# Low parts of the gate weights in the RWKV phase: subtraction moved from POOL to DVE

## The reference

```python
a_q, a_k, a_v, a_f, b_q, b_k, b_v, c_in, gate_in = _split_cols(h @ w_in, IN_SPLITS)
...
y_c, s_new = _rwkv7_scan(heads(cr), heads(decay), heads(kmod), heads(cv), kk, heads(a), rwkv_s0)
...
branches = jnp.stack([out_a, out_b, out_c], axis=2)
proj = jnp.einsum('btiw,iwd->btid', branches, w_branch)
gates = jax.nn.sigmoid(gate_in.reshape(b, t, N_BRANCH, D_MODEL))
y = jnp.sum(gates * proj, axis=2) @ w_out
```

## Time and profile before

| what | value |
|---|---|
| median of 3 runs | 3753.3 us (3747.02 to 3755.54) |
| the profiled execution | 3756.2 us, its span 3754.6 us |
| busy share of the span | PE 83%, PEld 75%, DVE 43%, ACT 18%, POOL 9% |
| mean granted PE clock | 0.866 of full speed |
| RWKV phase, first layer | from about 727 to 1093 us of the span |
| RWKV phase, second layer | from about 2574 to 2939 us |

### The profile page before, as it was taken

The page is one execution under the profiler, slowest core; times in us unless marked ns, Lnnn a source line. Parts: engine busy times, 40 slices in busy tenths (PEclk is TensorE's granted clock), DMA queues, the critical chain, the costliest instruction groups (busy, mean ns, idle before and its releaser), DMA issues.

```text
span 3754.6 us, 70050 instructions
## 1 busy us (share of the span) xinstructions
PE 3131.2 (83%) x26572; PEld 2818.4 (75%) x26572; DVE 1631.1 (43%) x3026; ACT 661.1 (18%) x1627; POOL 322.4 (9%) x388
## 2 busy tenths in 40 slices
PE   4995977599988797999969959676999787889997
PEld 3994544398887676999969935445988786679997
DVE  3342334355556325554353323333555552365533
ACT  1001323322221121000000023232222111300001
POOL 1001100022210001000000011001222000000000
PEclk8997566699998898999989955567999898989999
DMA  3442121222214212232224411203222332123221
GB/s 101 137 132 65 44 62 41 91 75 76 76 57 128 67 55 67 84 89 79 79 70 137 127 40 44 62 26 112 73 73 61 95 108 73 51 62 89 86 80 55
DMA packets 419279, 293.79 MB, mean 78 GB/s; under 512 B 37120, under 2 KB 384800, under 8 KB 418528
## 3 DMA queue, kind: packets, MB, share of 16 engines
q1 hardware_dynamic: 397056, 225.19, 21.4%
q0 software_dynamic: 21984, 65.35, 5.0%
HBM read 234.28 MB, written 56.23 MB: 77 GB/s over the span
## 4 chain that ended last, share of the span: by engine, by line
PE 72%; DVE 11%; DVEq 5%; issue 4%; ACT 3%; DMA 3%; ACTq 1%; POOLq 1%; SPq 0%; POOL 0%
PE PS L611 37%; PE PS L915 6%; PE PS L891 4%; PE PS L592 3%; PE PS L573 3%; PE PS L795 2%; ACT U L1169 2%; PE PS L694 2%; PE PS L1064 2%; PE PS L728 1%; PE PS L875 1%; DVE WLO L1623 1%; PE PS L980 1%; DVE hT L1603 1%; PE PS L1011 1%
## 5 line engine op out<-in xcount | busy, mean ns | idle before, releaser
L611 PE MATMUL PS<-U_r,WHI 128*128 128x272 f32 x3552 | 672.5, 293 | 93.9 <-DVEq L1624 26.1
L611 PEld LDWEIGHTS PS<-U_r,WHI 128*128 128x128 f32 x3552 | 540.3, 193 | 100.8 <-issue 60.0
L611 PE MATMUL PS<-hT_r,WHI 128*128 128x272 f32 x2656 | 550.9, 289 | 0.0
L611 PE MATMUL PS<-U_r,WLO 128*128 128x272 f32 x2592 | 544.9, 292 | 0.0
L1613 DVE CAST WHI<-ring 128x1024 fp32r<-128x1024 f32 (+2 forms) x278 | 180.0, 647 | 711.1 <-PE PS L611 697.6
L1172 ACT COPY U<-PS 128x272 f32<-128x272 f32 (+11 forms) x722 | 254.7, 370 | 1247.0 <-PE PS L611 453.7
L611 PEld LDWEIGHTS PS<-hT_r,WHI 128*128 128x128 f32 x2656 | 420.8, 190 | 0.0
L611 PEld LDWEIGHTS PS<-U_r,WLO 128*128 128x128 f32 x2592 | 416.1, 193 | 0.0
L611 PE MATMUL PS<-brT_r,WHI 128*128 128x272 f32 x1792 | 378.2, 293 | 19.2 <-DVE hT_r L1632 19.2
L1623 DVE TENSOR_TENSOR WLO<-ring,WHI 128x1024 fp32r<-128x1024 f32 (+2 forms) x278 | 315.0, 1133 | 20.9
L611 PEld LDWEIGHTS PS<-brT_r,WHI 128*128 128x128 f32 x1792 | 289.6, 193 | 20.0 <-DVE hT_r L1632 20.0
(11 more groups left out here) (299 smaller groups left out, 3858.0 us busy)
## 6 DMA issues: line engine op xcount, KB each, us to landing
ring<-in_w_in_dram SPq DMA_DIRECT2D x126, 512.0 KB, 3.9
ring<-in_w_ffn_in_dram SPq DMA_DIRECT2D x88, 512.0 KB, 3.8
proj_scratch<-U POOLq DMA_DIRECT2D x38, 544.0 KB, 4.2
ring<-in_w_ffn_out_dram SPq DMA_DIRECT2D x32, 448.0 KB, 3.5
U<-proj_scratch SPq DMA_DIRECT2D x48, 272.0 KB, 3.5
gate_scratch<-U POOLq DMA_DIRECT2D x96, 136.0 KB, 2.2
U<-gate_scratch SPq DMA_DIRECT2D x48, 272.0 KB, 2.8
ring<-in_w_branch_dram SPq DMA_DIRECT2D x48, 256.0 KB, 3.0
```

The costliest lines, as they stand in the source:

```text
L611: ins = mm(PS[:, 2 * q + h, 0:HT], w, half(x, h), start=(first and k == 0 and n == 0), stop=(last and k == kn - 1 and n == len(terms) - 1))
```

## The change

`gate_rest` is taken out of POOL's program and written into DVE's, with the same operands, the same wait for `gt_cast` and the same increment of `split_done`. POOL keeps the stores and their confirmation. On DVE the six subtractions of a pair stand in three places: unit 2 behind L1865, ahead of the wait for `rw_exps`; units 3, 4 and 5 behind the increments of `rw_ev` that follow L1880, ahead of the first `evac`; units 6 and 7 behind `rp_done` and `rw_gate_free`, at the end of the pair.

```diff
--- before.py
+++ after.py
@@ -1819,6 +1819,16 @@
                         L, LM = RTMP[:, 0, :], RTMP[:, 1, :]
                         EL, EN, EM = RTMP[:, 2, :], RTMP[:, 3, :], RTMP[:, 1, :]
 
+                        def gate_rest(n):
+
+                            v = V_GATE + 6 * p + n
+                            c = unit_of(v)
+                            hi, lo, w = (x.rearrange("p k n -> p (k n)")
+                                         for x in (WHI[:, v % 2, :, :], WLO[:, v % 2, :, :], ring[:, c % RING, :, :]))
+                            dve.wait_ge(gt_cast, l * 24 + it * 12 + 6 * p + n - 1)
+                            tt(lo, w, hi.bitcast(F32), ALU.subtract)
+                            dve.drain().then_inc(split_done, 1)
+
                         def dvec(name, i):
                             return VT[:, ds(it * 2 + (_v[name] + p + i), 1)]
 
@@ -1863,6 +1873,7 @@
                             ts(T0[:, c], PS[:, 2 + 2 * s, 0:TP // 2], 1e-24, 2.0 ** 20, ALU.max, ALU.mult)
                         dve.drain().then_inc(rw_clip, 1)
                         stt(T2, Rx, dvec("rwkv_rk", 0), T1, ALU.mult, ALU.mult).then_inc(rw_in, 1)
+                        gate_rest(2)
                         dve.wait_ge(rw_exps, g + 1)
                         copy(DCOL, EL.rearrange("p (c n) -> p c n", c=9)[:, :, CHUNK - 1])
                         tt(BEf, BEf, T0, ALU.mult)
@@ -1881,6 +1892,8 @@
                         dve.drain()
                         for gr in range(3):
                             dve.sem_inc(rw_ev[gr], 1)
+                        for n in (3, 4, 5):
+                            gate_rest(n)
 
                         def evac(s, gr):
                             X1, KA, HTt, X2, Ao, Vt, Kt, P4, Q8, M2, rt, Mst = PL[gr]
@@ -1963,6 +1976,8 @@
                         dve.memset(Kx[:, T:TP], 0.0)
                         dve.drain().then_inc(rp_done, 1)
                         dve.sem_inc(rw_gate_free, 1)
+                        for n in (6, 7):
+                            gate_rest(n)
                 phase_end(dve, l, 5)
 
 
@@ -2231,19 +2246,8 @@
                                 wait(gt_stored[h], 16 * (l * 24 + it * 12 + 6 * p + n + 1))
                             pool.sem_inc(gt_free, 1)
 
-                        def gate_rest(n):
-
-                            v = V_GATE + 6 * p + n
-                            c = unit_of(v)
-                            hi, lo, w = (x.rearrange("p k n -> p (k n)")
-                                         for x in (WHI[:, v % 2, :, :], WLO[:, v % 2, :, :], ring[:, c % RING, :, :]))
-                            wait(gt_cast, l * 24 + it * 12 + 6 * p + n - 1)
-                            pool.tensor_tensor(lo, w, hi.bitcast(F32), ALU.subtract)
-                            pool.drain().then_inc(split_done, 1)
-
                         for n in range(4):
                             gate_store(n)
-                            gate_rest(n + 2)
                             gate_kept(n)
                         wait(rw_fin, g + 1)
                         for h in range(2):
```

## The result

The changed kernel takes 3799.1 us in the median of four runs (3790.6 to 3801.4), the kernel before 3754.4 us beside it (3747.0 to 3762.3): a ratio of 1.0115, 95% interval [1.0088, 1.0141]. It is slower, as forecast, but by 44.7 us where 30.4 were predicted (3783.7, on the 3753.3 that stood ahead of the prediction), and 2 us above the end of the range. The profiled execution of the changed kernel took 3797.4 us, its span 3795.8 us, 41.2 us more than the span before.

The account below looks back on a forecast made before the run. TensorE was taken as the bound, so changes count only where it waits; 15.6 + 12.2 + 4.0 - 1.4 = +30.4 us on the 3753.3 us median gave 3783.7 us, range 3768 to 3797.

Parts of the forecast that it names:

- the relief: In DVE's head: without POOL's subtractions, 4.72 us less in second and fourth pairs, 2.5 us in the third.
- The terms for the six transitions: Between pairs: 15.6 us into pairs two and four, 12.2 into the third, 4.0 for TensorE's clock, over both layers.
- the clock: TensorE's matmuls behind the sums run slower after longer idling: 4 us in total over six transitions.
- The wait at the sums: TensorE's idle before the second pair's sums, waiting for DVE's squares, grows from 2.33 to 6.2 us.
- The idle of the loop's edge: DVE's 4.31 us idle at its loop's back edge, before the third pair's head, is still paid behind the wait.
- The clock term: TensorE from first to second sums takes 7.11 us in all six transitions, adding 4 us in total.
- rival C: gate_rest(5), before the first evacuation, delays TensorE's small matmuls: up to 10.4 us more, 3794 us; chance 12%.
- the first two places: Units 2 to 5 on DVE, behind L1865 and before the first evacuation, were taken to cost 0.
- A: Relief of DVE wins and its head starts earlier: at most 14 us plus 1.4 gained, 3738 us; chance 4%.
- At the end of a layer's phase: POOL finishes once its last store lands, with no head queued: 0.7 us gained, 1.4 in two layers.
- The stores and their confirmations stay: On POOL, only six subtractions of 2.40 us per pair are removed; earlier-free slots of GST give nothing on the path.

Follow-up runs that it names:

- e3: Changed kernel with units 6 and 7 subtracted on POOL again, units 2 to 5 left on DVE: 3757.3 us, ratio 1.0001 to the kernel before.
- e1: Changed kernel with unit 7 of each loop iteration's first pair subtracted behind the squares in the next pair's head: 3776.5 us, ratio 1.0047 to the kernel before.
- e7: The kernel before, unedited, run and profiled a second time: 3764.7 us in its one run.
- e5: Changed kernel with unit 5 subtracted later, where DVE waits for ACT, and one POOL drain per pair: 3793.2 us, ratio 1.0097 to the kernel before.
- e2: Changed kernel with a POOL drain added after each gate's stores, six times a pair: 3794.1 us, ratio 1.0094 to the kernel before.
- e4: Changed kernel with DVE's loop over the two iterations written out: 3792.5 us, ratio 1.0094 to the kernel before.
- e8: Changed kernel with units 6 and 7 in the next pair's head, DVE's loop written out, POOL drains after each gate: 3744.5 us, ratio 0.9960 to the kernel before.
- e9: Changed kernel, DVE's loop kept, unit 7 behind the next pair's squares, POOL drains after each gate: 3745.6 us, ratio 0.9961 to the kernel before.

## Why the prediction was wrong

**Right: which wait takes the place of the relief.** The forecast was that gate_rest(7) waits for ACT's cast and holds up the next head. Rows show it at L1829 with 4.82 us, e3 that nothing else in the edit costs time between the pairs, and e1 that the same work behind the squares, without the wait, is free.

**Right: the size of it, in part by luck.** The terms for the six transitions came to 31.8 us. From sums to sums they measure 30.85 us, but the clock behind the fourth pair's sums was in the terms too: from there to the last store it is 1.43 us more in the first layer and 0.09 in the second. So 32.4 us stand against 31.8. That is closer than two profiles of one kernel agree (1.5 us in e7). The parts agree less well: the last transition grew by 7.08 us, partly since the first profile of the kernel before had it at 85.3 us where e7 has 87.7. The wait at the sums was put at 6.2 us and is 5.99. The idle of the loop's edge was taken as 4.31 and is 3.56. The clock term holds where it can be read: from the second pair's sums to the last five half units 840.98 to 848.06, 7.08 us, where 7.11 was taken.

**Right: unit 5 (rival C) and the first two places cost nothing.** e3 has a ratio of 1.0001 with them on DVE, and moving unit 5 away (e5) changed no time in the small matmuls. In the first pair the first evacuation does start later behind the sums, 24.91 us (773.89) against 23.68 (768.07), 1.2 us as forecast, and the end of the small matmuls does not move with it. C is out, as is A: the cast lies 7 us behind rp_done, and cannot be passed.

**Wrong: the term "At the end of a layer's phase ... 0.7 us gained, 1.4 in two layers".** It took POOL to be done when its stores had landed, and put the drain at the barrier at nothing, without a reason. From the last store's issue to the next phase the trace has +3.98 us in the first layer and +4.0 in the second, so the term is +8.0 and not -1.4, a miss of 9.4 us. Of the 40.35 us by which the two RWKV phases grew, 30.4 were predicted; this term is nearly all of the rest. The step that failed is "The stores and their confirmations stay": it is true, but leaves out that the diff takes away not only POOL's subtraction but also the `pool.drain()` behind it. On POOL that drain had worked off what the stores left (that is inferred from e2 and e5; the barrier's own drain took 0.05 us before), hidden behind TensorE. Without it the 64 stores of a phase leave it all to the drain of the barrier, where everyone waits: 5.29 us. e2 shows that with drains in idle time the phase's end comes back by 4.5 and 5.7 us, and e5 that the price goes by the number of stores. With the drain out of the way the forecast's direction is right: in e2 it is 3.17 us from the last store's issue (1110.43) to the next phase (1113.60), 1.1 us less than the 4.28 before. With +8.0 in the term's place the working gives 30.4 + 9.4 = 39.8 us, 3793 us, inside the range.

The median missed by 15.4 us. Besides the 9.4, that is 0.6 in the transitions, 0.8 outside the phases, 3.5 between the median's difference (44.7) and the profile's (41.2), and 1.1 by which the kernel before was slower beside the changed one than ahead of the prediction. These 6 us lie within the scatter: four runs of the changed kernel spread over 11 us. That 3799.1 lies 2 us beyond the range rather than inside it hangs on them as well.

**Rows of before that could have told.** The drain behind POOL's subtraction in the kernel before, by line (ns, min/median/max):

```profile
L2242 POOLq DRAIN  x48: 2767/2890/4075, 743.6 to 2935.4; - x48
```

It lasts from its issue through the subtraction, 2.40 us, and 0.49 us more. That an operation stood there with a time of its own was to be seen, and the question was what it cleared and who pays when it is gone.

## What to carry to other kernels

A wait that moves from an engine with nothing behind it to one with the next stage behind it costs the next stage's start, whatever the work costs there: here 1.2 us of work was free in two places and cost 4 to 7 us a pair in a third. Put such work behind the instruction that hands over to the engine that bounds the kernel, and look also at what its semaphore releases: a slot freed later held up loads on SP that had nothing to do with it. Where an edit takes a drain away together with the instruction it followed, ask what else that drain had been clearing.

## What the hardware showed unexpectedly

- POOL's drain takes time for each store that POOL issued since its last drain, though these have landed: 0.206 us for two, 0.54 for six, 0.706 for eight, 1.352 for sixteen, 5.29 for 64, and 0.04 to 0.06 where none was issued in between. As an estimate from these, 0.04 us and 0.082 for each store. It goes by the count and not the bytes: in e2 four state stores of 16 KB add 0.33 us, as much for each as the gate stores of 136 KB.
- DVE's scan with two inputs in SBUF went from 1.35 to 3.62 us beside POOL's subtraction, which reads SBUF too, and is 1.35 us in all eight pairs without it. In the kernel before, POOL's subtraction starts 0.01 us ahead of the scan at 819.77:

```profile
819.76 2.40 POOL L2241 TENSOR_TENSOR WLO<-ring,WHI 128x1024 fp32r<-128x1024 f32 x1
```

  By the rule of the Trainium skill, "SBUF — State Buffer" (Who interferes with whom), either of the two holds the other off for a whole instruction. The trace agrees: the scan took 2.27 us more, against POOL's 2.40.
- DVE idles 3.3 to 4.6 us at its back edge in these profiles and 0.26 when the loop is written out (e4), without any new cost that the profile shows for the longer code. TensorE is idle there too, 1.5 to 3.0 us (1.53 before, 1.62 in e8, 3.03 in e9); that this is its own back edge is not tested.
